# Second product of the first layer: weight splits every second tile at its beginning, a filler tile ahead of the second scores, a norm ahead of a tile

## The reference, cut to what matters

```python
proj = hn @ w_in
rq, rk, rv, rg, nq, nk, nv = jnp.split(proj, [...], axis=-1)
rq, rk = rotary(rq, pos), rotary(rk, pos) * RET_DH ** -0.5
y = bidir_scan(rq, rk, rv, rv, a_f, a_b)            # decay by distance, both directions
mu = jnp.mean(y, -1); var = jnp.mean(jnp.square(y - mu), -1)
y = (y - mu) * lax.rsqrt(var + EPS) * ret_gn_g
ret_out = jax.nn.silu(rg) * y
na_out = neighborhood_attention(nq, nk, nv, na_rpb)  # softmax(q k + bias) v in 8 x 16 windows
return jnp.concatenate([ret_out, na_out], -1) @ w_out
```

## Time and profile before

| what | value |
|---|---|
| median of 3 runs | 1896.14 us (1895.11 to 1897.52) |
| profiled execution | 1892.94 us, its span 1891.2 us |
| PE busy | 1775.2 us, 94% |
| DVE busy | 1166.6 us, 62% |
| ACT busy | 769.8 us, 41% |
| mean granted clock | 0.976 |

### The profile page before, as it was taken

One profiled execution on the slowest core, in us unless ns is written; L12 is line 12 of the kernel. 1 busy time (PEld: TensorE's weight loads), 2 busy tenths in 40 slices (PEclk: granted clock), 3 DMA queues, 4 the chain that ended last, 5 costly groups with the idle time before them and its releaser, 6 DMA issues.

```text
span 1891.2 us, 20686 instructions
## 1 busy us (share of the span) xinstructions
PE 1775.2 (94%) x8194; PEld 1387.4 (73%) x8194; DVE 1166.6 (62%) x1591; ACT 769.8 (41%) x1310; POOL 178.7 (9%) x199
## 2 busy tenths in 40 slices
PE   7998989899999899999998899999979899999996
PEld 5886548677667688888876687767658688888885
DVE  4544665476666688664336998666774468766334
ACT  4235543254224444443223454555463345444220
POOL 0300300031000011110000000111220001111000
PEclk9999999989999999999998999999989999999998
DMA  5322002321112232333331222111003222332331
GB/s 207 95 94 67 1 0 90 122 78 56 57 55 89 68 101 91 99 101 97 94 104 62 78 90 78 34 34 45 25 10 100 79 89 92 98 100 91 99 93 64
DMA packets 42752, 147.86 MB, mean 78 GB/s; under 512 B 5153, under 2 KB 6305, under 8 KB 42529
## 3 DMA queue, kind: packets, MB, share of 16 engines
q1 hardware_dynamic: 39168, 138.43, 22.8%
q10 hardware_dynamic: 3488, 8.12, 1.2%
HBM read 144.44 MB, written 2.10 MB: 77 GB/s over the span
## 4 chain that ended last, share of the span: by engine, by line
PE 80%; DVE 12%; ACT 5%; issue 1%; DMA 1%; ACTq 0%; POOL 0%; DVEq 0%
PE bank L322 22%; PE bank L323 22%; PE bank L324 22%; DVE cv L1552 4%; DVE w_lo L291 2%; PE bank L1653 1%; PE bank L1104 1%; PE bank L1112 1%; ACT em L1753 1%; PE bank L657 1%; DVE bank L487 1%; PE bank L1614 1%; PE bank L1097 1%; PE bank L670 1%; PE bank L1635 1%
## 5 line engine op out<-in xcount | busy, mean ns | idle before, releaser
L322 PE MATMUL bank<-a_hi,w_hi 128*128 128x512 f32 x1504 | 608.1, 404 | 38.5 <-DVE a_lo L387 27.8
L291 DVE TENSOR_TENSOR w_lo<-raw,w_hi 128x1024 fp32r<-128x1024 f32 (+1 forms) x264 | 337.5, 1281 | 460.6 <-ACT w_hi L284 460.3
L323 PE MATMUL bank<-a_lo,w_hi 128*128 128x512 f32 x1504 | 591.3, 393 | 0.0
L324 PE MATMUL bank<-a_hi,w_lo 128*128 128x512 f32 x1504 | 590.8, 393 | 0.0
L284 ACT ACTIVATE w_hi<-raw 128x1024 fp32r<-128x1024 f32 (+1 forms) x264 | 274.7, 1044 | 452.6 <-DMA raw<-in_w_down 142.4
L322 PEld LDWEIGHTS bank<-a_hi,w_hi 128*128 128x128 f32 x1504 | 286.0, 190 | 117.8 <-issue 30.2
L323 PEld LDWEIGHTS bank<-a_lo,w_hi 128*128 128x128 f32 x1504 | 285.9, 190 | 64.9 <-issue 7.2
L324 PEld LDWEIGHTS bank<-a_hi,w_lo 128*128 128x128 f32 x1504 | 285.5, 190 | 60.6
L1013 ACT ACTIVATE u<-bank,par 128x512 f32<-128x512 f32 x88 | 68.5, 779 | 176.9 <-DVE bank L487 176.9
L322 PE MATMUL bank<-g_hi,w_hi 128*128 128x512 f32 x352 | 137.1, 389 | 0.0
L323 PE MATMUL bank<-g_lo,w_hi 128*128 128x512 f32 x352 | 137.1, 389 | 0.0
(11 more groups left out here) (347 smaller groups left out, 2082.4 us busy)
## 6 DMA issues: line engine op xcount, KB each, us to landing
raw<-in_w_up SPq DMA_DIRECT2D x88, 512.0 KB, 3.5
raw<-in_w_in SPq DMA_DIRECT2D x52, 512.0 KB, 3.5
raw<-in_w_out SPq DMA_DIRECT2D x32, 512.0 KB, 3.6
raw<-in_w_down SPq DMA_DIRECT2D x32, 512.0 KB, 3.5
raw<-in_w_xbc SPq DMA_DIRECT2D x24, 512.0 KB, 3.5
raw<-in_w_z SPq DMA_DIRECT2D x16, 512.0 KB, 3.5
raw<-in_w_down SPq DMA_DIRECT2D x16, 384.0 KB, 3.1
x<-in_xT ACTq DMA_DIRECT2D x4, 512.0 KB, 6.9
```

The costliest lines, as they stand in the source:

```text
L291: nc.vector.tensor_tensor(w_lo[:, q % RING, 0:w], raw[:, q % RING, 0:w], w_hi[:, q % RING, 0:w].bitcast(F32), ALU.subtract).then_inc(lo_do ...
L322: nc.tensor.matmul(out, wh, rhs_hi[:, k, :], start=k == first, stop=False)
L323: nc.tensor.matmul(out, wh, rhs_lo[:, k, :], start=False, stop=False)
L324: return nc.tensor.matmul(out, wl, rhs_hi[:, k, :], start=False, stop=stop)
```

## The change

`split_ahead` for the second product: slot 8 ahead of tiles 0 and 1, 9 ahead of 2 and 3, 10 ahead of 4 and 5, 11 ahead of 6 and 7, then t + 4 as before. In step 0 of the neighbourhood attention, tile 8 goes ahead of the scores of step 1 on TensorE, and its split and evacuation ahead of the shift of step 1 on VectorE. In the odd retention steps, the norm goes from behind the tiles to ahead of them.

```diff
     def split_ahead(name, t):
-        return PLAN[name]["slot0"] + max(min(t, 4 if name == "in2" else 5) + 8, t + AHEAD) if name in SUMS else last_slot(name, t) + AHEAD
+        if name == "in2":
+            return PLAN[name]["slot0"] + (8 + t // 2 if t < 8 else t + AHEAD)
+        return PLAN[name]["slot0"] + max(min(t, 5) + 8, t + AHEAD) if name in SUMS else last_slot(name, t) + AHEAD
...
         for s in range(NA_STEPS):
-            if s + 1 < NA_STEPS:
+            if 0 < s < NA_STEPS - 1:
                 na_scores(pe, s + 1)
             tile_pe(pe, "in2", 8 + s, a_hi, a_lo)
+            if s == 0:
+                na_scores(pe, 1)
...
             if s:
                 turned(s - 1)
+            if s == 0:
+                tile(8)
             if s + 1 < NA_STEPS:
                 for e in range(2):
                     shift(s + 1, e)
                 invert(s + 1, 0)
-            lo_to(dve, split_ahead("in2", 8 + s))
+            if s:
+                lo_to(dve, split_ahead("in2", 8 + s))
             if s + 1 < NA_STEPS:
                 invert(s + 1, 1)
-            take(8 + s)
+            if s:
+                take(8 + s)
...
             if half == 0 and p:
                 keep_ret(p - 1)
+            if half and p:
+                norm(p - 1)
             for n, t in enumerate(RET_TILES[r]):
...
-            if half and p:
-                norm(p - 1)
```

## The result

The median of four executions is 1882.74 us (1881.18 to 1884.52), beside 1895.66 for the kernel before. The ratio is 0.9925, with a 95% interval of 0.9912 to 0.9938: 14.2 us less, 11.8 to 16.7. Applied to the 1896.14 us from which the prediction started it gives 1881.9 us, where 1886.5 was forecast and the range ended at 1882.5. The direction was right and the gain larger than the range allowed.

What follows compares the result with a forecast made beforehand. TensorE, busy 94% of the span, was taken as the bound, so only its waits and slow clock pay. Gains of 9.3 us less 2.6 for the clock, plus 2.9, make 9.6: 1896.14 to 1886.5 us, range 1882.5 to 1891.0.

Steps and rivals of the forecast that it cites:

- Part 1: Second product, splits every second tile: tile 7 out at 371.0 instead of 377.87, gain 6.9 us, idle time 2.3 us.
- Part 2: Tile 8 ahead of step 1's scores: removes a 2.19 us wait, adds 4.0 us idle ahead of step 2's scores.
- The clock: Lower clock behind TensorE's two remaining gaps: 0 lost behind the 2.3 us gap, 2.6 us behind the 4.0 us gap.
- the first idle time: TensorE's 2.3 us gap ahead of the first windows: clock loss taken as 0, bounds 0 and 1.5 us.
- the nearest row: Earlier profile: after 3.83 us idle the clock ran at 0.51 for 5.2 us, priced as 2.6 us lost.
- the stretch: From tile 7's end to step 0's values product, 32.0 us before; the forecast for it is given as 25.3 us.
- the free-running monitor: Skill's rule that slow matmuls vary between runs; claimed to allow any median between 1883.8 and 1886.5 us.
- rival 2: Clock falls in both gaps, making the chain 1.5 us longer: 8.1 us gained, 1888.0 us; chance 0.2.
- Part 3: Odd retention steps, norm ahead of the tiles: 3.08 us wait ahead of the third product goes, gain 2.9 us.
- The sum: Whole kernel: 6.7 us from the attention stage plus 2.9 from the norm move, 9.6 us, median 1886.5 us.
- The range: Whole kernel's median: 1882.5 to 1891.0 us, including a microsecond or so for scatter between medians.
- rival 1: Clock stays up in the second gap, ahead of step 2's scores: 12.2 us gained, 1883.9 us; chance 0.13.

Runs made afterwards that it cites:

- the idle time filled: Changed kernel plus 8 and 16 overwritten 512-column matmuls in TensorE's two idle times, ahead of the first windows and step 2's scores: 1879.40 us, ratio 0.9913.
- the second profile: The changed kernel measured again with nothing altered, beside the kernel before: median 1885.20 us, ratio 0.9942.

## Why the prediction was right or wrong

**Part 1.** Right. Tile 7 out at 370.90 (forecast 371.0), the first windows at 370.95, the idle time 1.99 us (2.3).

**Part 2.** The order and the chain were right: tile 8 at 372.87 (372.6) and the scores of step 2 at 384.75 (384.7), named as what is late next. The idle time ahead of them was 2.3 us (2.9 and 2.8 in the other profiles), not 4.0, since TensorE itself was later: it ended the turning at 382.4, not 380.7, most of it by tile 8's 7.0 us in place of 5.66. That part 2 costs 1.1 to 2.1 us once part 1 is there was not seen; the prediction gave one gain for both together. Its own sum held a reason: the 2.3 us for slot 12's two halves.

**The clock.** This step was wrong in both its terms, and they partly cancel. In the first idle time I took no fall; in three profiles of three it fell, after 2.0 to 2.15 us idle, which cost the chain 0.3 to 0.9 us (from the first windows to the first shift 2.0, 2.6 and 2.6 us, where it was 1.75 with the idle time filled). The rest fell on tile 8, hidden beside the chain. In the second I took 2.6 us from the nearest row; it was 1.6 (scores and tile 9 took 393.07 - 384.75 = 8.3 us where 6.7 is full clock, and the second profile has the same 8.3). Forecast for the stretch: 25.3 us; measured 24.1, 24.9 and 24.8. The stage gained 7.5 us in the mean of the profiles, against 6.7. The sentence that puts the median between 1883.8 and 1886.5 by the free-running monitor doesn't follow from the prediction's own sums: they give 1883.9, and up to 1888.0 where the clock falls in both gaps (rival 2), which is what it did.

**Part 3.** Right to 0.1 us: 2.9 us gained, the wait of 0.84 grown to 1.06 (forecast 1.1), nothing gained or lost in the odd steps before it.

**The sum.** By the traces 7.5 + 2.9 = 10.4 us, against 9.6. By the times, 14 executions of the changed kernel in three measurements have a mean of 1885.0 us and the 45 of the kernel before beside the experiments one of 1896.3: 11.3 us, with a standard error of 0.7. That error takes the executions as independent; the three measurements by themselves gave 14.2, 11.0 and 9.5. The forecast of 1886.5 is 1.5 us off.

**The range.** This is the step that failed: "with a microsecond or so for the scatter between medians". The first four executions gave 14.2 us by their ratio, the next five 11.0, the last five 9.5; on either of the later two the range would have held, so the draw decided. No trace of the changed kernel has a gain beyond rival 1's 12.2: the two stages gave 10.8 us in the first profile, and its whole span was 11.7 us shorter. So what the range lacked was room for scatter and not a mechanism. Executions of one kernel are spread by 3 to 9 us in a measurement (1892.63 to 1901.10 for the kernel before), with a standard deviation of 1.4 to 2.1 us for the changed one, and they follow the mean granted clock: of the kernel before, the 13 executions at 0.976 took 1892.5 to 1895.3 us, the 7 at 0.973 took 1896.8 to 1899.0. The rows at hand said so: the profiled execution was 3.2 us under the median, and I carried a difference from it over to the median as if that offset were fixed. The three medians of the changed kernel, of four and five executions, lie 4.7 us apart; 2.5 us on each side of their middle hold them, so with hindsight the range should have begun near 1881.4 us, 2.5 under rival 1. Whether chips differ too in what this change gives isn't settled: the three ratios come from different measurements, and the intervals of the first and the last only touch.

## What to carry to other kernels

When a wait is removed, sum the chain that decides next on all its engines, and look at what the edit itself put into it: here the split that was moved out of one wait went into the next, and moving it once more, or leaving the filler tile out, gave 1 to 4 us in the trace. Before a range is written, look at how far the profiled execution is from the median: that distance hints at what one draw is worth. Measure a stage between two of its own events: profiles of one kernel then agreed to 0.1 us where the clock fell in the same way and to 0.8 us where it didn't, while the medians moved by 4.7.

## What the runs showed of the hardware

The granted clock fell behind shorter idle times than I had priced: 1.99, 2.15 and 2.09 us in the three profiles of the changed kernel, while 3.08 us in the earlier trace rows left it up. The prediction had a row for it, 0.57 behind 2.35 us of idle time, and set it aside. The same wait of 2.35 us was followed by 0.66 in one kernel and 1.00 in another. So the length of an idle time alone doesn't tell whether the clock falls. Matmuls whose result is thrown away, put into idle time, kept it up: two fills of 1.97 and 3.91 us took 1.5 to 2.3 us out of the stage. The Trainium skill (TensorE: Matmul & The Clock Gate, Part 1: The HAM clock gate) says that the monitor's window runs free and isn't reset when a kernel starts. The traces are consistent with it, since the same instructions behind the third product took 1267.2 to 1272.1 us with 55.3 to 71.8 us at the lower clock; that a free-running window is the cause is shown by no run here.
